# A hybrid decoder step on one Trainium2 core: in Strassen units the matmuls of A11 and S1, and of S2 and S4, alternate between two PSUM banks, and two copies and one sum are issued earlier

## The reference, cut to what matters

```python
def swiglu(x, w_gu, w_down):
    g, u = jnp.split(x @ w_gu, 2, axis=-1)
    return (jax.nn.silu(g) * u) @ w_down

h = x + 0.5 * swiglu(rms_norm(x, w['g_ffn1']), w['w_ffn1_gu'], w['w_ffn1_down'])
...                                   # GLA and S5 mixer, cross attention
h = h + 0.5 * swiglu(rms_norm(h, w['g_ffn2']), w['w_ffn2_gu'], w['w_ffn2_down'])
```

## Time and profile before

| | us |
|---|---|
| time, median of 3 runs | 1280.26 (1280.12 to 1280.7) |
| time of the profiled execution | 1278.66 |
| its span | 1276.8 |
| PE busy | 1263.2 (99%) |
| DVE busy | 858.3 (67%) |
| ACT busy | 531.3 (42%) |
| POOL busy | 354.2 (28%) |
| mean granted TensorE clock | 0.996 |

### The profile page before, as it was taken

One profiled execution on the slowest core, in us unless ns is written; L12 is line 12 of the kernel. 1 busy time (PEld: TensorE's weight loads), 2 busy tenths in 40 slices (PEclk: granted clock), 3 DMA queues, 4 the chain that ended last, 5 costly groups with the idle time before them and its releaser, 6 DMA issues.

```text
span 1276.8 us, 24146 instructions
## 1 busy us (share of the span) xinstructions
PE 1263.2 (99%) x10181; PEld 1222.8 (96%) x10181; DVE 858.3 (67%) x1062; ACT 531.3 (42%) x803; POOL 354.2 (28%) x411
## 2 busy tenths in 40 slices
PE   8999999999999999999999999999999999999998
PEld 8999999999999999999899997699999999999997
DVE  5986479847985637468565437479995589637953
ACT  7553145421224422574433323246552255314543
POOL 0036633288993211000002100032330133102321
PEclk9999999999999999999999999999999999999998
DMA  6223223263223532125332756322333323322322
GB/s 194 84 83 100 83 86 97 84 137 92 83 62 89 103 82 52 51 83 155 104 100 83 261 195 221 99 83 67 100 100 85 98 83 100 96 82 88 88 63 75
DMA packets 221085, 129.95 MB, mean 102 GB/s; under 512 B 22257, under 2 KB 213281, under 8 KB 220961
## 3 DMA queue, kind: packets, MB, share of 16 engines
q1 hardware_dynamic: 217664, 123.86, 34.1%
q10 hardware_dynamic: 3312, 4.54, 1.1%
HBM read 121.42 MB, written 5.78 MB: 100 GB/s over the span
## 4 chain that ended last, share of the span: by engine, by line
PE 94%; DVE 3%; ACT 1%; issue 1%; DMA 1%; SPq 0%; DVEq 0%; ACTq 0%
PE PS L744 91%; PE PS L1386 1%; DMA raw<-in_w_ffn_gu 1%; ACT gua L1674 0%; PE PS L1472 0%; DVE xl L2159 0%; PE PS L1363 0%; DVE AR L2802 0%; PE PS L976 0%; PE PS L868 0%; ACT Xs L1945 0%; DVE PS L2148 0%; DVE PS L2141 0%; ACT wh L1525 0%; DVE ARr L2154 0%
## 5 line engine op out<-in xcount | busy, mean ns | idle before, releaser
L1525 ACT ACTIVATE wh<-raw 128x1024 fp32r<-128x1024 f32 (+1 forms) x126 | 130.1, 1032 | 375.7 <-PE PS L744 375.0
L744 PE MATMUL PS<-yh,wh 128*128 128x288 f32 x960 | 206.0, 296 | 0.0
L744 PE MATMUL PS<-yh,wl 128*128 128x288 f32 x960 | 205.0, 295 | 0.0
L744 PE MATMUL PS<-yl,wh 128*128 128x288 f32 x960 | 205.0, 295 | 0.0
L2047 DVE TENSOR_TENSOR wl<-raw,wh 128x1024 fp32r<-128x1024 f32 (+1 forms) x126 | 154.9, 1230 | 63.6 <-ACT wh L1525 62.2
L744 PE MATMUL PS<-xh,ARr 128*128 128x288 f32 x792 | 174.2, 297 | 0.4 <-ACT sq L1608 0.2
L744 PE MATMUL PS<-xh,wh 128*128 128x288 f32 x736 | 163.7, 304 | 0.6 <-DVE xl L2359 0.6
L744 PE MATMUL PS<-xh,wl 128*128 128x288 f32 x736 | 157.7, 296 | 0.0
L744 PE MATMUL PS<-xl,wh 128*128 128x288 f32 x736 | 157.3, 295 | 0.0
L744 PEld LDWEIGHTS PS<-yh,wh 128*128 128x128 f32 x960 | 154.1, 188 | 1.5 <-DVE yl L2727 0.8
L744 PEld LDWEIGHTS PS<-yl,wh 128*128 128x128 f32 x960 | 154.4, 188 | 0.0
(11 more groups left out here) (381 smaller groups left out, 2191.5 us busy)
## 6 DMA issues: line engine op xcount, KB each, us to landing
raw<-in_w_ffn_gu SPq DMA_DIRECT2D x88, 512.0 KB, 3.8
raw<-in_w_ffn_down SPq DMA_DIRECT2D x32, 512.0 KB, 4.0
raw<-in_w_in SPq DMA_DIRECT2D x16, 512.0 KB, 4.0
raw<-in_w_ckv SPq DMA_DIRECT2D x16, 512.0 KB, 3.8
raw<-in_w_ffn_down SPq DMA_DIRECT2D x16, 384.0 KB, 3.4
Hs<-in_cache_mem_k SPq DMA_DIRECT2D x6, 1024.0 KB, 6.2
raw<-in_w_out SPq DMA_DIRECT2D x8, 512.0 KB, 4.0
raw<-in_w_cq SPq DMA_DIRECT2D x8, 512.0 KB, 5.2
```

Of the source, the lines that this page charges most:

```text
L744: return e.matmul(out, lhsT, rhs, start=start, stop=stop, **kw)
L1525: e.activation(wh[:, n % 2, 0:K * P], raw[:, n % 4, 0:K * P], ACT.Copy).then_inc(w_hi, 1)
```

## The change

`two_products` issues two products in turn, a matmul of the one into its bank and then a matmul of the other into the other bank, and lets both report at the end. Units that are first in their group stay as they are. In the other 28 units A11 and S1 become one such pair of 24 matmuls, S2 and S4 another. All waits of both products stand ahead of the pair. On ScalarE the copy e5 moves ahead of `high_gate`, which then follows both copies. On VectorE the up sum of the previous unit moves from `finish` to right behind `low_last`.

```diff
+            def two_products(v, j0, b0, h0, l0, j1, b1, h1, l1, begins=True):
+                for k in range(HK):
+                    for wi, (low, x0, x1) in enumerate(((0, h0, h1), (0, l0, l1), (1, h0, h1))):
+                        at = dict(start=begins and k == 0 and wi == 0, stop=k == HK - 1 and wi == 2, skip_group_check=True)
+                        one = mm(bank(b0, TH), operand(v, j0, low)[:, k, :], x0[:, k, :], **at)
+                        other = mm(bank(b1, TH), operand(v, j1, low)[:, k, :], x1[:, k, :], **at)
+                one.then_inc(S("pr_done"), 1)
+                other.then_inc(S("pr_done"), 1)
...
-                product(v, A11, U, xh[:, lo, lo_t], xl[:, lo, lo_t])
                 if first:
+                    product(v, A11, U, xh[:, lo, lo_t], xl[:, lo, lo_t])
...
                 e.wait_ge(S("t1_lo"), base + HK)
-                product(v, S1, 2, tok_h[:, :, 0, :], tok_l[:, :, 0, :])
-                if not first:
+                if first:
+                    product(v, S1, 2, tok_h[:, :, 0, :], tok_l[:, :, 0, :])
+                else:
+                    two_products(v, A11, U, xh[:, lo, lo_t], xl[:, lo, lo_t], S1, 2, tok_h[:, :, 0, :], tok_l[:, :, 0, :])
                     product(v, A12, 1, xh[:, hi, lo_t], xl[:, hi, lo_t])
...
+                else:
+                    e.wait_ge(S("e_ok"), 4 * v + 2)
+                    two_products(v, S2, U, tok_h[:, :, 2, :], tok_l[:, :, 2, :], S4, 2, xh[:, hi, hi_t], xl[:, hi, hi_t], begins=False)
...
                 keep(v, 1, e1, u_bank(v))
-                high_gate(after(v)) if after(v) else conv(units[v] + 2)
+                if v in FIRST_UNIT:
+                    high_gate(after(v))
                 if v:
                     e.wait_ge(S("c_ok"), 2 * v)
                 keep(v, 3 if v in FIRST_UNIT else 2, e5, 2, scale=-1.0)
+                if v not in FIRST_UNIT:
+                    high_gate(after(v)) if after(v) else conv(units[v] + 2)
                 high_sums(after(v)) if after(v) else conv(units[v] + 3)
...
                     low_last(v)
+                    if going:
+                        up_sum(v - 1)
                     if nxt:
                         for j in (S2, S3, S4):
                             sum_of(j, nxt)
```

## The result

| | before | after |
|---|---|---|
| time, median of 4 runs each, us | 1280.19 (1279.48 to 1280.7) | 1288.22 (1287.54 to 1290.09) |
| ratio to before | | 1.0068 [1.0053, 1.0083] |
| time of the profiled execution, us | 1278.66 | 1287.69 |
| its span, us | 1276.8 | 1285.8 |

The changed kernel is slower by 0.68%, 9.03 us between the two profiled executions and 8.03 between the medians (whose plain quotient is 1.0063; it lies in the interval). The forecast was 1295.9, that is 15.6 slower. The time lies in the range of 8 in 10 (1278 to 1301) and under the forecast's own range (1291 to 1301): the sign and the place were as worked out, the size was 1.7 times too large by the profiled executions and 1.9 times by the medians. One execution of experiment 1 took 4375.46 us, for no known reason, and is left out of its ratio.

What follows compares the result with a forecast made beforehand. TensorE was taken to bound the kernel, with VectorE's round as long; blocked rounds add 16.5 us, removed stalls take 0.9, so 1280.26 + 15.6 = 1295.9. Own range 1291 to 1301, 8 in 10 1278 to 1301; chance 0.60.

Steps and rivals of the forecast that it cites:

- TensorE bounds, and VectorE has no room: TensorE busy 99% of the span; VectorE's round, 11.17 us, is as long as TensorE's and hidden only by its lead.
- The S3 sum's block: VectorE's S3 sum, held up by GpSimd's shorter subtraction, loses its 0.52 us block once the up sum moves ahead.
- The removed stalls: TensorE's stalls of 0.33 in unit 1, 0.47 in unit 13 and 0.11 in units 14 to 18 go: -0.9 us.
- The round: VectorE's loop from gate sum to gate sum, with the product with the gate blocked 2.13: 11.95 us for 11.13, +0.82 per unit.
- The tie: GpSimd's request at 5.2 us after the gate sum, against the product with R's start at 5.25; either order gives 11.95.
- The first overrun: Unit whose gate sum first comes late, such as unit 6: 0.34 late, 0.06 restart, 0.1 first matmul, 0.5 us before the next.
- Sum in the units: Longer rounds over the five groups, 3.8, 3.8, 2.1, 4.7 and 2.1: 16.5 us, less 0.9 of removed stalls.
- The plain blocks and what follows them: Blocks behind a group run at 133.3 or 130.0 ns by how it ends: -5 to +1.3 us, only in the range.
- No block: Rival: product with the gate gets in ahead of GpSimd, TensorE bounds, old stalls go: 1279.4 us, chance 0.16.
- Its variant with 130.0 ns: Rival: no block, and alternating matmuls also run at 130.0 ns: another -3.4, 1276.0 us, chance 0.10.
- One unit in three: Rival: the product with the gate is blocked in only a third of units: +4.6, 1285 us, chance 0.09.
- the longer round: Rival: each hand-over between the four engines costs 0.1 more, round 12.35: +23.6, 1303.9 us, chance 0.05.

Runs made afterwards that it cites:

- e1: Changed kernel, GpSimd's longer subtraction replaced by one zero fill that reads nothing (low parts of A11 and A12 left out): 1276.12 us, 0.9982 of the kernel before.
- e2: Changed kernel, GpSimd's longer subtraction also waits until the product with the gate is done, nothing left out: 1277.33 us, 0.9993 of the kernel before.
- e4: Changed kernel, ScalarE's `high_gate` moved ahead of the copies e1 and e5, so GpSimd asks earlier: 1296.74 us, 1.0146 of the kernel before.
- e9: Changed kernel, GpSimd's longer subtraction replaced by three zero fills in a row (low parts of A11 and A12 left out): 1275.1 us, 0.9967 of the kernel before.
- e5: Changed kernel with TensorE's order and waits of before, keeping ScalarE's and VectorE's new order: 1283.81 us, 1.0035 of the kernel before.
- e8: Changed kernel, TensorE's order of before except S2 and S4 alternating in each group's last unit; GpSimd waits for the product with the gate: 1275.82 us, 0.997.
- e3: Changed kernel, each pair's products issued one bank after the other, same waits and reports: 1292.39 us, 1.0118 of the kernel before.
- e6: Changed kernel, GpSimd's longer subtraction waits for the product with the gate, and pairs run one bank at a time: 1281.32 us, 1.0016 of the kernel before.
- e10: Changed kernel, TensorE's order wholly as before, no alternation; GpSimd's longer subtraction waits for the product with the gate: 1279.32 us, 0.9995 of the kernel before.
- e7: Kernel before, only S2 and S4 alternating in each group's last unit, S4's wait for e5 ahead of both: 1286.68 us, 1.0062 of the kernel before.

## Why the prediction was right, and where it was off

**Held, by its own steps.** TensorE bounds, and VectorE has no room: yes, the chain moved to VectorE as soon as its round grew. The S3 sum's block goes: 0.68 for 1.21. The removed stalls go (unit 1, unit 13, units 14 to 18). In unit 5 nothing is blocked; its gate sum ends 10.54 into the unit (10.67 forecast). In unit 6 the product with R starts at 4.52 (4.79), GpSimd asks at 5.05 (5.03), and the product with the gate takes 2.84 (2.89). Both come out in all groups, and e1, e2, e4 and e9 show that the block is GpSimd's reading and that the 19 waits hang on it. The alternation brings nothing in the units: 84 matmuls in 11.16 us in units without a stall, where it was 11.13; the 132.5 ns that I took is 132.8, and the 0.03 of a unit lies in the products behind a pair, below.

**The round: 11.95 worked out, 11.76 measured.** This is the term that was mis-sized. With the gate sum's end as 0 (1090.96 in the rows above):

| | forecast | measured |
|---|---|---|
| product with R starts | 5.25 | 5.14 |
| it ends | 6.01 | 5.89 |
| GpSimd ends | 8.31 | 8.15 |
| product with the gate ends | 8.93 | 8.76 |
| next gate sum ends | 11.93 | 11.75 |

Of the 0.18, 0.10 is one number: I took 0.77 us from the up sum to the next start, since the earlier trace rows have it so. There the next instruction, the product with R, reads what the up sum wrote. In the new order the S2 sum follows, which doesn't need it, and starts after 0.67 (1093.63 to 1094.30); `low_sums`, which doesn't need the product before it, followed that after 0.68 in the earlier trace rows as well. Another 0.04 is the hand-over, below; the rest is hundredths. The tie was none: GpSimd's record starts at 5.38, 0.24 behind the product. Seventeen rounds are 17 x 0.19 = 3.2 us of the difference.

**The first overrun: 0.5 worked out, 0.4 measured**, three times: 0.26 to 0.30 in unit 6 (21, 29), and 0.11 that is left in the last unit of a group, mostly the slower first matmul. Unit 5's gate sum is 0.13 earlier than worked out and the round 0.2 shorter, so the gate sum of unit 6 ends 11.13 into it, not 11.47. It still stalls TensorE, by 0.23, for the restart takes longer than the 0.06 that I had from a copy by ScalarE: here 0.25 from the gate sum's end to the first matmul (1090.96 to 1091.21). By the same longer restart, units 0 and 12 grew by 0.67 and 0.73, where 0.5 and 0.56 were worked out with the first matmul in them. In a steady round the restart costs nothing: GpSimd starts by the end of the product with R and not by its own request, 0.37 before, so VectorE's loop doesn't pass through TensorE.

**Sum in the units.** Forecast 16.5 less 0.9; measured 12.68 net, that is 13.6 and 0.9.

**The plain blocks and what follows them: 0 taken, -3.39 measured.** The prediction named this ("-5 to +1.3 over all", by how a group ends) and left it in the range. By the runs it is a term with a sign: an alternating last pair gives 130.0 ns. Together with 0.26 of an earlier start this is the larger half of the difference: 2.9 in the units, 3.65 outside, together the 6.6.

**The rivals.** No block (1279.4) is refuted by L2214 at 2.84. Its sum can be held against e2, in which the block is taken out: 0.9993, as 1279.4 is 0.9993 of 1280.26. But that is luck, for the terms are others: the five groups are not 0.9 shorter but 1.5 longer (two waits left, 0.03 in each other unit), and faster plain blocks make up for it. Its variant with 130.0 ns was partly right, for the blocks and not for the units: e1 and e9, without the block, are at 0.9982 and 0.9967, and 1276.0 was worked out, which is 0.9967. One unit in three is refuted by the nineteen waits, the longer round by 11.76. The change does what it says, and still what it was to remove (0.9 us of stalls) is smaller than what one displaced subtraction brings.

## What to carry to other kernels

An engine with no slack has a round of its own; before a wait is moved ahead of some work, close that round over itself with the new times, and look which operation falls onto a reading GpSimd. Cover eaten by a too long round only delays the cost, so a cost that is hidden by a lead must be followed over many rounds (e5). And where a change is half good, undo the bad half before giving up: here the cure was a wait more, on the engine that had time.

## What the runs showed of the hardware

- **Only a reading GpSimd blocks.** Beside GpSimd subtractions of 2.4 us, VectorE operations with two SBUF operands grew by up to 2.08 (L2214) and 2.23 us (L2164 in e4); beside three writes of 0.96 us each, none grew (e9). Operations with one operand in PSUM never did (`low_sums` 1.75 and 1.76). The Trainium skill (SBUF — State Buffer, "Who interferes with whom") has a two-input tensor-tensor operation contend with GpSimd's reads; the traces agree.
- **The hand-over goes to the one that waits.** GpSimd asked during L2212 and was served ahead of L2214, though L2214 followed by 0.03 us. By its end less the unhindered 2.40, it began, by estimate, at 1099.11 - 2.40 = 1096.71, 0.14 before L2212's recorded end; I had put it 0.1 before. Its record starts 0.08 us behind `high_gate`, when it asks, so its 2.77 hold the waiting. In unit 21 of e5 the same estimate gives 1048.09 + 2.66 - 2.40 = 1048.35, 0.13 before the recorded end of the product with the gate.
- **Plain blocks know two paces.** Behind the units 3, 11, 18 and 26, the same matmuls run at 130.0 ns or at 133.3. With an alternating last pair in the group's last unit and no stall right in front of it they ran at the faster pace, 24 of 24 (after, e1, e2, e4, e8, e9). With one bank at a time (e3, e5, e6, e10), or with a stall in front (e7), at the slower, 20 of 20. The kernel before keeps to that behind units 3, 11 and 26, and breaks it behind unit 18, at 130.0. Behind unit 11 the faster pace ends after four blocks, where other work is put in between, and behind unit 32 it is never there.
- **The pace is there before the blocks start.** In the last unit of a group S3, twelve matmuls into one bank with the same code in all kernels, runs at 133.3 to 133.4 ns in each of the 25 cases in which the faster blocks follow, that of the kernel before behind unit 18 too. In the other 23 it runs at 131.6 to 131.7. So what runs slower in the unit runs faster in the blocks, and this is also the 0.03 us by which a unit with pairs is longer. What is set there, and why it stays for hundreds of matmuls, isn't known; no run here was made to tell.
- **A first matmul after a wait costs more**: 0.21 us to the next start (1091.21 to 1091.42) where 0.13 is usual.
- **A restart takes 0.05 to 0.26 us, and the engine that releases it doesn't decide.** From VectorE's gate sum it is 0.26 at the head of a unit, in all waits of the changed kernel, e3 and e4. In e5 it is 0.10 at S1 and 0.05 or 0.06 at the first plain block behind units 3, 11 and 18. From a copy of ScalarE it is 0.05 in the earlier trace rows and 0.14 in unit 18 of e7 (964.74 to 964.88). What in the place in the program makes it was not tried.
